# A rewritten instruction order for the third block of a three-block layer: same instructions, another sequence on four queues

## The reference

```python
def hybrid_layer(x, ...):
    hn = rms_norm_3(x, norm_gain)
    proj = hn @ w_in                       # 17 column groups: q, k, v, gates, forget
    o_fox  = forgetting_attention(rms(fq), rms(fk), fv, log_sigmoid(ff + b))
    o_moba = moba_attention(rms(mq), rms(mk), mv, rel_bias)
    o_sb   = stick_breaking_attention(sq, sk, sv)
    o_swa  = swa_sink_attention(rms(wq), rms(wk), wv, sinks, rel_bias)
    y = concat(o_fox * silu(fg), o_moba * silu(mg), o_sb * silu(sg), o_swa * silu(wg))
    return x + y @ w_out
```

## Time and profile before

| | |
|---|---|
| median of 3 runs | 3597.68 us (3595.95 to 3602.85) |
| the profiled execution, its own time | 3602.85 us |
| its span in the trace | 3601.1 us |
| third block in the span: last loads begin, first product, first closing product, end | 3182.50, 3222.84, 3554.08, 3601.1 us |
| PE busy over the whole span | 87% |
| DVE, ACT busy over the whole span | 67%, 39% |

### The profile page before, as it was taken

How to read it: one execution, slowest core, us unless ns; L and a number is a source line. 1 busy time by engine, 2 the same in 40 slices (tenths; PEclk the granted TensorE clock), 3 DMA queues, 4 the chain that set the end, 5 groups by cost and what they waited for, 6 DMA issues and landing times. The chain is left out here.

```text
span 3601.1 us, 34659 instructions
## 1 busy us (share of the span) xinstructions
PE 3133.6 (87%) x11816; PEld 2000.1 (56%) x11816; DVE 2412.6 (67%) x4718; ACT 1396.8 (39%) x2336; POOL 711.3 (20%) x583
## 2 busy tenths in 40 slices
PE   8988889987787778777788999998499999959999
PEld 4655644433333333333356787786388888837667
DVE  4877456667766776677658545554588888854565
ACT  2324322222222222222243233333378888843563
POOL 0000023444444444444400000000112222100000
PEclk9989899999999999999999999999699999969999
DMA  8322169999999999999942222232699999932112
GB/s 283 113 82 88 47 245 392 395 395 422 418 410 422 415 415 417 419 413 410 418 159 62 65 71 68 71 107 89 221 344 372 375 371 369 367 111 65 47 36 71
DMA packets 351924, 905.63 MB, mean 251 GB/s; under 512 B 29953, under 2 KB 170753, under 8 KB 285570
## 3 DMA queue, kind: packets, MB, share of 16 engines
q0 software_dynamic: 84000, 549.52, 37.3%
q1 hardware_dynamic: 267746, 353.85, 29.1%
HBM read 896.45 MB, written 31.99 MB: 258 GB/s over the span
## 5 line engine op out<-in xcount | busy, mean ns | idle before, releaser
L258 PE MATMUL peer_acc<-peer_uv,peer_diag 128*128 128x512 f32 x2048 | 997.5, 639 | 237.9 <-ACT peer_diag L314 232.2
L435 DVE CUSTOM_DVE_ANT_0 peer_uv<-peer_uv,firsts_h 128x1024 f32<-128x1024 f32 x512 | 627.5, 1227 | 346.8 <-DMA peer_uv<-in_peer_uv,peer_experts 345.1
L258 PEld LDWEIGHTS peer_acc<-peer_uv,peer_diag 128*128 128x128 f32 x2048 | 408.5, 204 | 808.1 <-issue 490.2
L210 POOL DMA_INDIRECT peer_uv<-in_peer_uv,peer_experts x512 | 587.2, 1147 | 1217.1 <-PE peer_acc L258 700.7
L3066 DVE TENSOR_TENSOR slotted_low<-slotted_raw,slotted_high 128x2048 fp32r<-128x2048 f32 x192 | 434.1, 2288 | 66.8 <-ACT slotted_high L3015 66.8
L3015 ACT ACTIVATE slotted_high<-slotted_raw 128x2048 fp32r<-128x2048 f32 x192 | 365.6, 1920 | 65.0 <-PE slotted_h L2972 51.0
L314 ACT ACTIVATE peer_diag<-all_consts,peer_weights 128x128 f32<-128x128 f32 x512 | 166.4, 391 | 333.4 <-DVE peer_weights L428 305.7
L305 ACT ACTIVATE peer_act_in<-peer_act_in 128x4 f32<-128x4 f32 (+1 forms) x130 | 26.6, 205 | 609.2 <-DVE peer_act_in L435 609.2
L2972 PE MATMUL slotted_h<-slotted_high,slotted_xT_high 128*128 128x512 f32 x512 | 205.1, 401 | 6.2 <-DVE slotted_low L3066 4.1
L2972 PE MATMUL slotted_h<-slotted_high,slotted_xT_low 128*128 128x512 f32 x512 | 201.9, 394 | 0.0
L2972 PE MATMUL slotted_h<-slotted_low,slotted_xT_high 128*128 128x512 f32 x512 | 201.7, 394 | 0.0
(11 more groups left out here) (752 smaller groups left out, 5663.4 us busy)
## 6 DMA issues: line engine op xcount, KB each, us to landing
slotted_raw<-in_moe_w SPq DMA_DIRECT2D x192, 1024.0 KB, 11.0
mixers_raw<-in_w_in SPq DMA_DIRECT2D x56, 512.0 KB, 3.8
firsts_ada_raw<-in_w_ada SPq DMA_DIRECT2D x64, 256.0 KB, 2.8
third_raw<-in_w_in SPq DMA_DIRECT2D x30, 512.0 KB, 3.8
firsts_raw<-in_w_in SPq DMA_DIRECT2D x28, 512.0 KB, 4.2
firsts_ada_first<-in_w_ada SPq DMA_DIRECT2D x8, 1024.0 KB, 14.2
peer_uv<-in_peer_uv,peer_experts POOLq DMA_INDIRECT x512, 10.8
ffn_w_raw<-in_peer_wq SPq DMA_DIRECT2D x10, 512.0 KB
```

The source lines that it names most:

```text
L210: pool.indirect_dma_start(uv[:, n % R, :, :].rearrange("p a d -> p (a d)"), None, A["peer_uv"], bass.IndirectOffsetOnAxis(ap=experts[:, si ...
L258: mm = nc.tensor.matmul(acc[t % 2][j][:, :], diag[:, n % 4, :], uv[:, n % R, 1, j * BANK:(j + 1) * BANK], start=(m == 0), stop=(m == E - 1))
L435: nc.vector.tensor_tensor_reduce(uv[:, n % R, 0, :], uv[:, n % R, 0, :], h2[:, t, :], 1.0, 0.0, ALU.mult, ALU.add, act_in[:, side, i:i + 1 ...
```

## The change

The change replaces the four strings of `THIRD_ORDER`. Each engine gets the same number of steps of every stream as before (tensor 8 a, 305 b, 41 c, 144 d, 40 e; and so on), so every instruction, every wait and every buffer is the same, and only the sequence on a queue differs. Nothing else in the program is touched.

```diff
 THIRD_ORDER = {
     "sync": (
-        "b2 a38 c2 a c6 "),
+        "b2 a39 c8 "),
     "tensor": (
-        "a8 b10 c b8 c b8 c b7 c b3 c b3 c2 b10 c2 b2 d2 b6 c b8 c5 b8 c b d b d b5 d2 b d e b4 d b3 d b d b5 d2 "
-        "b d e2 b d2 b d b4 d2 b d b d2 b d b d2 c b d b d2 b d b d2 b d b d2 b d b d2 c2 d e2 d2 b d b d2 b d b "
-        "d2 e d b4 c b8 c e2 b e2 b e b6 c b15 e4 b c e c4 b2 c b8 d2 b2 e2 d e2 d2 c e d c d2 c d c d2 b d b d2 "
-        "b d b e2 d2 c e d b e d2 b d b e d2 b5 d b d2 b d b d2 b d b e4 d2 b d b e d2 c2 b2 d b d2 b d b2 d2 b d "
-        "b d2 b d b e3 d2 c d c e b e d2 b7 d b d2 b d b d b d b d b d2 b d b d b d b4 d b d b d c d c d2 b d b "
-        "d2 b d b d b d b d b d2 b d b d b d b d b d2 b d b d2 b d b d2 b d b3 d2 b d b d2 b d b d e2 d e2 c2 b64 "),
+        "a8 b11 c b8 c b7 c b7 c b3 c b5 c3 b c2 b d2 b9 c5 b3 d b d b2 d2 b c d b3 d2 b d b4 d b d b d b5 d2 b d "
+        "b3 d2 b d b d2 b d b d b d e d b d2 b3 d b d2 b d b d2 b d c b2 d2 b d b d2 b d b d e d b d b c b d2 e2 "
+        "d e b2 e b9 c b5 c b3 e4 b e b9 c b c b7 e2 b2 e2 c2 e c3 b d2 b2 d b d2 b6 c b d b d2 b d b d2 b d b3 "
+        "d2 e d e3 c3 d2 e b6 d b d2 b2 d b2 c d2 b d b d b d c d b d2 e b2 d e b d e2 d b d c2 d2 b d b d b d b "
+        "d c e c d2 b5 d b d2 b2 d b2 d2 b d b d2 b d b d2 b d b3 d2 b d b d e d b d b d b2 d b d b d2 e3 d b d2 "
+        "b d b e d c2 d b d b d b d b d b d2 b4 d b d b d b2 d b d2 b d b d e d b2 d b d2 e3 d b e d2 b8 d b d b "
+        "d b2 d3 e4 c2 b64 "),
     "scalar": (
-        "a13 b a3 b a4 c b c b c b c b e c b f2 c b c b c e b c e b e g c g2 b g c b h g3 b c g h g h2 g b g c g4 "
-        "b g2 e c g6 b g2 e c g5 h g b c h b h2 c h e b c b c h3 b h e c e c h g2 h2 b g2 h g6 h c g h g h e g b "
-        "g h g2 c g2 b h g2 h2 g2 h g2 c g2 b h g3 c g h2 b g2 e h g2 c g b g4 c g d g2 h g2 c b2 g7 c g b g6 c g "
-        "b g5 e g h2 e2 c d e2 b e2 b e b5 "),
+        "a3 b2 a17 b c b c b c b c b e c b f c e f b c e2 g3 b c g3 b g c g2 b g c g4 b g c g2 h g3 b g c g2 e g2 "
+        "h g2 b g h c g e g h g h b c b c h4 b2 c2 e h b h2 c h g2 e g2 b c e g2 b g h g c g2 h3 g2 b g2 c g b g "
+        "c g2 h e g2 h2 g3 b g c g2 h g2 b g2 c e g4 b c g2 h g3 h b g c g3 h g3 b h g2 c g2 d g2 b g2 h g c g b "
+        "g2 h c g h g h g2 b g2 b g c2 d e h e h2 e5 b e b5 "),
     "vector": (
-        "a23 b a2 b5 c d b d c d c b c2 b3 c3 e2 c b e c e b e2 f5 b f e f e f3 e2 b e6 b e8 b e3 f e2 f e2 f5 b "
-        "f5 b f7 b f2 b f3 c f2 b c3 f8 c e f2 e c f e f b e c e f e f e f2 e f e f4 e f c e f e2 f e b e f3 e f "
-        "e f3 e f e f e f b f e f e c e f3 e f e f3 e f e2 b e2 f2 c2 e b e f2 c e f3 e f e2 b e2 f e2 f e f2 c "
-        "e2 f2 e b e2 b e2 c e c e c e2 c e b e6 b e5 c2 e c3 f c f c4 b c7 b3 g4 b3 g4 "),
+        "a8 b2 a17 b5 c d c b c3 d2 b c e2 c e c e b e c e3 b c e2 b e5 b e3 f2 e f e3 b e f2 e f2 e f e2 f e b e "
+        "f e2 f3 b f4 b f8 b2 f9 c b f2 c4 e f2 e f e f2 b f e f e2 f e b e f2 e c e f2 c2 e f2 e f e b e f3 e2 b "
+        "e f2 e f e f e c e2 f e2 b e f c e c2 e f2 e f e b e f e2 f e f2 e2 b e f e2 f e3 b e f e2 f e2 f c e b "
+        "f2 e f e f2 e f e f2 e c e b e3 f e b e f e f e f c2 e c f2 e f e b e b e f7 c4 f c f c11 b c b2 g4 b3 "
+        "g4 "),
 }
```

## The result

| | before | after |
|---|---|---|
| median of 6 runs each | 3602.33 us (3595.95 to 3602.85) | 3619.91 us (3618.37 to 3625.39) |
| ratio, 95% interval | | 1.0056 [1.0044, 1.0069] |
| the profiled execution, its own time and span | 3602.85, 3601.1 us | 3623.54, 3621.8 us |

The time lies inside the range, and slower was right. The size, 17.6 us between the medians, is close to the 17.0 forecast, but one term of that sum, the middle, failed. The ratio of 1.0056 isn't that of the two medians (1.0049); by it the change is 20 us, as in the two traces.

The account below looks back on a forecast made before the run. The third block was taken as the rows stage until the first product, then 375 us of nearly gapless PE work. Terms +7.0, +0.5 and +9.5 us sum to +17.0 on 3597.68, giving 3614.7 us, range 3603 to 3622.

Parts of the forecast that it names:

- the middle: First to last projection: same instructions, only switches and waits differ; +0.5 us, with ends of -4 and +7.
- The start: Rows stage to first product: ACT stands at two roundings awaiting loads, delaying the first product; +7.0 us, lower end 2.2.
- The two landings: Rows stage: loads of pieces 0 and 1 land at 3204.4 and 3206.1 us, as in the old trace.
- the closest chain: Second inversion of the norms (root, reciprocal, spread): needs about 7.5 us, PE has 8.5 us of other work, just fits.
- +0.7 for more switches: PE changes matmul kind 320 times instead of 313, with costly leaves from products 97 instead of 90: +0.7 us.
- The change-over: Last projection to closing products: last exponentials stand behind ACT's second Silu, PE idles, clock drops; +9.5 us, ends 0 and 11.
- The rule weighed: ACT's table loads at the tail: the skill page's drain would add 2.8 us, giving 3617.5; the sum used the trace row.
- Only the start: Rival: PE's remaining work hides the last exponentials, so only the delayed first product costs; 3605.2 us, chance 0.11.
- only the change-over: Rival: loads land earlier than read, so the first product is delayed by only 2.2 us; 3609.9 us, chance 0.08.
- The middle slips: Rival: tight places between the projections become three dips with waits and slow clock; 3621.2 us, up to 3625, chance 0.12.
- Faster: Rival: earlier softmax work spreads PE's waits between the projections and removes its dip; 3595.9 us, chance 0.04.
- nothing: Rival: the new sequence moves work inside slack everywhere in the third block; 3597.7 us, chance 0.05.

Follow-up runs that it names:

- e1: New kernel with the roundings and low parts of pieces 0 and 1 put back late, as before the change: 3621.0 us, ratio 1.0041 to the old kernel.
- e2: Old kernel with only the new order of the rows stage on ACT and DVE: 3607.02 us, ratio 1.0011 to the old kernel.
- e3: New kernel with the weight loads of pieces 0 and 1 issued earlier, ahead of the biases: 3618.92 us, ratio 1.0044 to the old kernel.
- e5: New kernel with DVE's last stick-breaking step moved ahead of the closing pieces' low parts and the totals: 3621.41 us, ratio 1.0057 to the old kernel.
- e7: New kernel with a product step between PE's second and third spreads and, on ACT, a projection copy ahead of a rounding: 3617.64 us, ratio 1.0048.
- e9: New kernel with old start, both moves between the projections, ACT's and DVE's last stick-breaking work earlier, totals ahead of the second low part: 3608.18 us, ratio 1.0014.
- e11: New kernel with one ACT move, a projection copy ahead of the rounding that waits for a product: 3621.71 us, ratio 1.0048 to the old kernel.
- e4: New kernel with ACT's last exponentials and their copies ahead of the last gates and second Silu: 3617.86 us, ratio 1.0038 to the old kernel.
- e10: New kernel with one PE move, a product step between the second and third of three spreads: 3620.12 us, ratio 1.0045 to the old kernel.

## Where the prediction held, and the step that failed

**The start** (forecast +7.0, measured +6.20): right in mechanism and nearly in size. The two landings carried the term, and e1, e2 and e3 show it three ways: back it costs nothing, alone it costs 6.4, with earlier loads 2.2. Most of the 0.8 us too much lie in the landing: I had it 21.9 us behind the block's first load, as in the one trace; in the new kernel the rounding began 21.2 us behind it (3204.68 - 3183.44). The term isn't sharper than that: in the nine executions with the new start and the loads in their place it began 20.8 to 21.7 us behind, and the first product came at 46.2 to 46.9; with the old start it came at 40.3 to 41.2.

**The middle** (forecast +0.5, measured +4.46): this is the step that failed, "I price the middle at +0.5 us". Its ends, -4 and +7, hold the value, and its mechanism, closer producers with a dip behind the wait, was named, but new waits were put at nothing on the ground that the closest chain "just fits". The runs split the 4.46 us. Without any dip behind the first 20 us the new sequence takes 326.03 us (e5) and the old one 324.01 (e2): 2.0 us, of which PE's recorded waits between the projections explain 1.7 (4.1 against 2.4 us). The dips cost 4.0 us in the new kernel (330.02 - 326.03) and 1.55 in the old one (325.56 - 324.01): 2.45 us more. These are differences of single executions, and the clock behind the first product shifts them by some tenths.

The chain that I had called the closest, the second inversion, did fit: its spread doesn't wait in the new kernel, and it waits 0.34 us where PE comes earlier (e7, e9, e11). The two new waits stand where I priced nothing. One, of 0.8 us, is at the first inversion, and not for root or reciprocal but for a PSUM bank that DVE hasn't read yet. The other, of 1.7 us, is the same pattern as at the start: on ACT a rounding that waits stands ahead of a square that PE needs. I looked for it only where the diff was easy to read. Whether the forecast's +0.7 for more switches is real stays open: e7, with the new kernel's switches but for the one step, is 0.26 us above e2, but it misses 0.6 us less clock right behind the first product, so 0.9 us would be left if that were equal.

**The change-over** (forecast +9.5, measured +9.06): right in mechanism and in size. The exponentials and the mask came 0.3 us later than worked out, since the rounding behind T began at T + 0.26. PE idled 6.34 us ahead of L3991 ("some 6"), the clock behind it was 0.68 rather than near 0.5, which over 5.4 us is 1.7 us, the term as it was taken. Forecast was 13.5 plus 1.7 of clock, 15.2 us in all; 14.74 came, and up to 15.74 in executions of the same order. What the prediction said on DVE, ready at T + 6.9 and so not the later one, was right too (T + 7.3), and it explains why e4 moved the transposes by only 1.1 us and the stage by 0.66.

*The rule weighed.* In the kernel after, activations follow the start of a table load by 1.30 us (3562.58, then 3563.88) and 1.29 us (3566.33, then 3567.62), and the first load starts where the activation ahead of it ends (3561.49 + 1.08). That is the row's price; the drain of the Trainium skill's page "ScalarE: Activation LUTs", section "What ACT_TABLE_LOAD costs", doesn't show in this chain either.

**The level.** In the traces the block grew by 19.76 us where 17.0 were forecast: 4.0 too few in the middle, 1.2 too many at start and change-over. The medians differ by 17.6 us, since the profiled execution of the new kernel lies 3.6 us above its median. Of the 5.2 us between 3614.7 and 3619.91, 4.65 come from the base: the median of three runs was 3597.68, that of six 3602.33. That 17.0 and 17.6 lie so close is luck in good part: the errors of the terms go against each other, and the traces and the ratio put the change at about 20 us.

**The rivals.** "Only the start" and "only the change-over" fall: both came, and e1 and e2 separate them. "The middle slips" came in part, with two places instead of three (its own sum, three times 0.7 + 1.4, is 6.3 and not 6.5). "Faster" and "nothing" needed an engine that passes a wait of its own queue; nowhere in these traces does one.

What stays open: why the clock dips in some executions and not in others of the same sequence, and why a dip can come 16 us behind a pause; the runs show that the sequence with both pauses loses more clock, and not how. The change-over's new order wasn't tried alone in the kernel before.

## What to carry to other kernels

In a queue executed in order, an instruction that waits for a load costs whatever stands behind it: read the landing time of that load before moving it forward, and look for the same instruction at every place of the sequence, not only where the diff is large. A tail has several engines close together; when one gate is removed, read which is second (here DVE, ready 0.34 us before ACT) and which is third before pricing the gain. And compare stages by marks in the trace, because the start of a stage can vary by more than the effect.

## What the runs showed of the chip that I had not expected

- The start of the block, after the same code, lay between 3176.9 and 3186.8 us in fourteen profiled executions of kernels that are the same up to there.
- In the sequence with pauses of PE of 0.8 and 1.7 us, six of seven executions lost 5.1 to 6.8 us of clock and the seventh none, which made 4.0 us in the time. With either pause removed, 0 or 1.7 us of clock were missing (one execution each).
- Taking a pause away need not give its length back: of 1.7 us at L3705 only 0.3 were left some 12 us later (e11 against e5).
- A dip can stand without a pause ahead of it: +56 us behind the first product in e10 and e9 (clock 0.59 and 0.60), PE busy 4.00 of 4 us in that window.
